# The first attention begins with five of eight projection chunks, and the other three are projected inside its rounds

## The reference, cut to what matters

```
proj = h @ w_in                                   # h: 256 x 1024
qa, kca, vca, ksa, vsa, kwa, vwa, ga, qb, kb, vb = split(proj)
o_a = nsa_attention(qa, kca, vca, ksa, vsa, kwa, vwa, sigmoid(ga), ...)   # compressed + selected + window
o_b = swa_sink_attention(qb, kb, vb, sinks, tab_b)                       # 8 heads, window, sinks
y   = concat(o_a, o_b) @ w_out
```

## Time and profile before

| | us |
|---|---|
| time, median of 3 runs | 1233.58 (1231.28 to 1238.41) |
| time of the profiled execution | 1230.09 |
| its span, first to last instruction | 1228.2 |
| PE busy | 1144.4 |
| DVE busy | 948.5 |
| ACT busy | 602.0 |
| POOL busy | 77.1 |

### The profile page before, as it was taken

How to read it: one execution, slowest core, us unless ns; L and a number is a source line. 1 busy time by engine, 2 the same in 40 slices (tenths; PEclk the granted TensorE clock), 3 DMA queues, 4 the chain that set the end, 5 groups by cost and what they waited for, 6 DMA issues and landing times.

```text
span 1228.2 us, 19517 instructions
## 1 busy us (share of the span) xinstructions
PE 1144.4 (93%) x8036; PEld 1026.6 (84%) x8036; DVE 948.5 (77%) x1638; ACT 602.0 (49%) x1055; POOL 77.1 (6%) x110
## 2 busy tenths in 40 slices
PE   2697899999999998999999999999999979999996
PEld 1696579899997996898998989999989968888885
DVE  5997758888777965788888678897776868777655
ACT  2435755443456457644444664444453265555553
POOL 1020000000000000285000000000000000000000
PEclk9999899999999999999999999999999999999998
DMA  9994235788982951377899637889723542666731
GB/s 374 364 390 166 94 138 194 303 325 283 336 323 72 409 223 58 118 270 261 319 242 361 224 123 285 312 279 330 299 94 119 108 181 88 225 253 259 182 124 35
DMA packets 41097, 280.74 MB, mean 229 GB/s; under 512 B 4768, under 2 KB 5296, under 8 KB 8240
## 3 DMA queue, kind: packets, MB, share of 16 engines
q1 hardware_dynamic: 37584, 269.27, 60.1%
q0 software_dynamic: 2416, 7.92, 2.0%
q10 hardware_dynamic: 1008, 2.30, 0.5%
HBM read 277.85 MB, written 1.10 MB: 227 GB/s over the span
## 4 chain that ended last, share of the span: by engine, by line
PE 72%; DVE 16%; ACT 6%; DMA 4%; issue 1%; SPq 0%; DVEq 0%; ACTq 0%
PE PS L419 71%; DVE LO L1433 5%; DMA raw<-WS 4%; DVE raw L1423 3%; ACT HI L987 2%; ACT SC L987 1%; DVE TMP L1502 1%; DVE HB L1497 1%; ACT SQ L987 1%; PE PS L642 1%; DVE TMP L1539 1%; ACT HB L987 1%; DVE X L1544 1%; DVE TMP L1774 1%; ACT RS L987 0%
## 5 line engine op out<-in xcount | busy, mean ns | idle before, releaser
L419 PE MATMUL PS<-HB,HI 128*128 128x256 f32 (+1 forms) x3160 | 650.3, 299 | 26.1 <-ACT HB L987 18.4
L419 PEld LDWEIGHTS PS<-HB,HI 128*128 128x128 f32 x3160 | 512.0, 193 | 52.5 <-ACT HB L987 20.9
L419 PE MATMUL PS<-HB,LO 128*128 128x256 f32 x1748 | 495.6, 284 | 0.0
L1433 DVE TENSOR_TENSOR LO<-raw,HI 128x1024 fp32r<-128x1024 f32 x340 | 406.1, 1231 | 93.5 <-ACT HI L987 93.2
L987 ACT ACTIVATE HI<-raw 128x1024 fp32r<-128x1024 f32 x340 | 338.4, 1047 | 92.5 <-PE PS L419 48.4
L419 PEld LDWEIGHTS PS<-HB,LO 128*128 128x128 f32 x1748 | 336.5, 193 | 2.9
L1423 DVE CUSTOM_DVE_ANT_0 raw<-raw,CB,SM 128x1024 f32<-128x1024 f32 x168 | 211.5, 1293 | 15.9 <-DMA raw<-WS 15.9
L987 ACT ACTIVATE HDH<-FB 128x256 fp32r<-128x256 f32 x88 | 36.8, 418 | 233.1 <-DVE FB L1621 209.5
L419 PE MATMUL PS<-HI,HDH 128*128 128x512 f32 x352 | 140.2, 398 | 0.0
L419 PE MATMUL PS<-HI,HDL 128*128 128x512 f32 x352 | 139.4, 396 | 0.0
L419 PE MATMUL PS<-LO,HDH 128*128 128x512 f32 x352 | 139.1, 395 | 0.0
(11 more groups left out here) (234 smaller groups left out, 919.9 us busy)
## 6 DMA issues: line engine op xcount, KB each, us to landing
raw<-WS SPq DMA_DIRECT2D x255, 1024.0 KB, 5.4
SC<-scratch POOLq DMA_DIRECT2D x2, 1024.0 KB, 16.3
FB<-gates_out POOLq DMA_DIRECT2D x3, 512.0 KB, 4.5
SQ<-gates_out POOLq DMA_DIRECT2D x3, 512.0 KB, 9.1
X<-xT ACTq DMA_DIRECT2D x1, 1024.0 KB, 6.7
SC<-ssm POOLq DMA_DIRECT2D x2, 512.0 KB, 3.8
out<-TMP SPq DMA_DIRECT2D x4, 256.0 KB, 2.6
CB<-vecs SPq DMA_DIRECT2D x1, 512.0 KB, 6.4
```

The costliest lines, as they stand in the source:

```text
L419: return e.matmul(o, l, r, start=start, stop=stop, skip_group_check=True)
L1433: e.tensor_tensor(LO[:, s % HL, :], raw_half(j, h), HI[:, s % HL, :].bitcast(fp32), O.subtract).then_inc(*D.up(("lo", s)))
```

## The change

Chunks 4, 5 and 6 leave the row of projections. What is begun with is ab 0, 1, 2, 3 and 7; the scores of rounds 0 to 5 need no more. The three others are projected in six halves, `third_set(p)`, in rounds 0 to 5, on PE behind the transposes of that round, into the PSUM banks 2 and 3, which no other step uses at that time. Each of the three engines calls `use(..., 2)` for that half in the round, DVE ahead of `spare` and of its `compressed` functions. The scores of round 6 wait for the new event `third`. The value columns of chunks 6 and 7 change places. In the plan `cmp` moves to place 19, behind ab 7; ab 4, mod 14, ab 5, mod 15, ab 6, mod 16 to 19 and `abo` follow it.

```
-    plan += weave(ws("ab", 8), am[:7], 0) + [("raw", ("cmp", 0))] + am[7:] + ws("abo", 4)
+    plan += weave([("w", ("ab", i)) for i in (0, 1, 2, 3, 7)], am[:6], 0) + [("raw", ("cmp", 0))]
+    for i in (4, 5, 6):
+        plan += [("w", ("ab", i)), am[i + 2]]
+    plan += am[9:] + ws("abo", 4)
...
-                w.wait_ge(*A.at(("fm", tag)))
+                w.wait_ge(*A.at(("fm", tag) if tag == "cd" or p < 6 else "third"))
...
-            for n in range(6):
+            for n in range(4):
                 linear_fm(("ab", n), H2, "ab", 8, 2)
-            keys_values(("ab", 6))
             values_only(("ab", 7))
+
+            def third_set(p):
+
+                key, h = ("ab", 4 + p // 2), p % 2
+                ps = PS[:, 2 + p // 2 % 2, :]
+                wt = [x.rearrange("p (k n) -> p k n", k=8) for x in weight(key, h)]
+                if p == 4:
+                    w.wait_ge(*A.at(("proj", "ab", 4)))
+                if p == 5:
+                    linear_tm(lambda qt: ps[:, 256 + qt * 128:384 + qt * 128], key, 1, range(8), wt, False, True)
+                else:
+                    for k in range(8):
+                        i = mm3(ps[:, h * 256:(h + 1) * 256], [x[:, k, :] for x in wt], H2[k], k, h == 0 and k == 0,
+                                k == 7, "ab")
+                    i.then_inc(*P.up(used(key, h), *([("lin", key, 0)] if h else [])))
...
                 if p > 1:
                     transposes("ab", p - 2)
+                if p < 6:
+                    third_set(p)
                 walk.spare(2)
                 for f in compressed.get(p, ()):
                     f()
... ACT
+            use(("ab", 7), 0, 2)
+            use(("ab", 7), 1, 2)
+            values(("ab", 7), 0, ("fm", "ab"))
+
+            def third_set(p):
+
+                use(("ab", 4 + p // 2), p % 2, 2)
+                ps = PS[:, 2 + p // 2 % 2, :]
+                if p in (1, 3):
+                    w.wait_ge(*P.at(("lin", ("ab", 4 + p // 2), 0)))
+                    fn(flat(FMT[:, p + 3:p + 5, :]), ps, F.Copy, scale=0.125).then_inc(*A.up(("proj", "ab", 4 + p // 2)))
+                if p == 5:
+                    w.wait_ge(*P.at(("lin", ("ab", 6), 1)))
+                    fn(FMT[:, 12, :], ps[:, 0:256], F.Copy).then_inc(*A.up())
+                    fn(VT[:, :, 256:384], ps[:, 256:512].rearrange("p (q n) -> p q n", q=2), F.Copy) \
+                        .then_inc(*A.up("third"))
...
                 for i in (2 * p, 2 * p + 1):
                     exps("ab", i, *AB[i])
+                if p < 6:
+                    third_set(p)
                 high(walk.spare(2))
... DVE
                 if p > 0:
                     scaled("ab", AB, p - 1)
+                if p < 6:
+                    use(("ab", 4 + p // 2), p % 2, 2)
                 low(walk.spare(2))
                 for f in compressed.get(p, ()):
                     f()
```

More of the change, by code:

```diff
@@ L1178, in act @@
             fn(HDH[:, 0, 0:192], S("gate"), F.Copy).then_inc(*A.up("gatew"))
-            for n, i in enumerate((4, 5, 0, 1, 2, 3)):
+            for n, i in enumerate((4, 5, 0, 1)):
                 use(("ab", n), 0)
@@ L1688, in dve @@
                 .then_inc(*D.up("gatew"))
-            for n in range(6):
+            for n in range(4):
                 use(("ab", n), 0)
                 use(("ab", n), 1)
-            for n in (6, 7):
-                use(("ab", n), 0)
-                use(("ab", n), 1)
+            use(("ab", 7), 0, 2)
+            use(("ab", 7), 1, 2)
             w.wait_ge(*P.at("gates2"))
@@ L2277 @@
     r = np.r_
-    abc = [r[512:640, 640:768, 768:896, 1024:1152], pairs, 1304 + pairs, r[1816:1944, 896:1024, 1152:1280, 1944:2072]]
+    abc = [r[512:640, 640:768, 768:896, 1024:1152], pairs, 1304 + pairs, r[1816:1944, 1944:2072, 896:1024, 1152:1280]]
     cdc = [pairs, r[768:1280], r[1280:1792], r[1792:2304], r[512:640, 640:768]]
```

## The result

The changed kernel takes 1243.07 us, median of 6 runs (1241.9 to 1245.58), beside 1234.05 us (1231.28 to 1238.41, 6 runs) for the kernel before. The ratio is 1.007 with an interval of [1.005, 1.0089]: about 9 us slower. The profiled execution took 1245.58 us with a span of 1243.8. An event of one execution also carries scatter: in six kernels that have the same instructions up to `cmp_used` (the changed one, bias_first, filled_wait, spread_mods, spread_and_bias_first and abo_half_moved) the first score begins between 78.7 and 80.9 us and `cmp_used` falls between 98.8 and 101.8.

What follows compares the result with a forecast made beforehand. PE and DVE were taken as full ahead of the attention, a chain of latencies as bounding the rounds. −18.4 + 7.1 + 3.9 + 8.4 + 3.0 = +4.0 us gave 1234.1 profiled, 1237.6 median; range 1228 to 1244.

Steps and rivals of the forecast that it cites:

- the sign of the sum: The five steps up to the end of round 6's scores add to +4.0 us, so slower.
- the likeliest case: Whole kernel follows the five-step schedule: 1237.6 us, own range 1233.5 to 1241.5; chance 0.50.
- Low clock on top: Rival: PE's waits in rounds 4 and 5 put the last projection half at low clock; 1239.5 to 1243, chance 0.20.
- The 3.5 us that I added: Added to the profiled execution's forecast of 1234.1 us to reach the median of the runs, 1237.6.
- Step 1: Start to first score: first score at 78.7 us, 18.4 us earlier than before.
- Step 2: First score to `cmp_used`: 20.4 us, 7.1 more, with three projection halves of 2.9 us on PE.
- Step 3: `cmp_used` to the end of `cmp_bias(0)`: 13.1 us, 3.9 more, with landing, low parts, mod 16 and bias.
- Step 4: To the end of `cmp_bias(1)`: 8.4 us more, six modulation halves 7.25 and a low part 1.15 on DVE.
- Step 5: `cmp_bias(1)` to the end of round 6's scores: 9.9 us, 3.0 more, including the last projection half at 5.3.
- Mod 19 lands by then: In round 4, five chunks behind `cmp_used` land within 15 us; mod 19 is wanted 21 us behind it.
- Behind the rounds: After round 6's scores: no change counted, with bounds 0 and −2.4 us for less DVE work.
- Faster: Rival: only PE's work counts and gaps in the rounds take it; −5 to −10 us, 1224 to 1229, chance 0.15.

Runs made afterwards that it cites:

- bias_first: Changed kernel with DVE's compressed functions of rounds 3 and later put ahead of `use` and `spare`; 1230.14 us, ratio 0.9988.
- filled_wait: Changed kernel with 20 matmuls of 512 columns, result unread, in PE's wait ahead of round 5's transposes; 1235.43 us, ratio 1.0023.
- spread_mods: Changed kernel with two modulation halves ahead of round 4's bias instead of six, four in round 5, no `abo` half in either; 1229.38 us, ratio 0.9981.
- spread_and_bias_first: Changed kernel with the edits of spread_mods and bias_first together; 1228.08 us, ratio 0.996.
- abo_half_moved: Changed kernel with the first `abo` 0 half moved from round 4 to round 5, the six modulation halves staying; 1245.66 us, ratio 1.0062.
- projection_left_out: Changed kernel with the projections of rounds 0 to 5 doing only the first of eight blocks of the feature sum; 1234.54 us, ratio 1.0023.
- modulation_cut_short: Changed kernel with DVE's modulation of mod 14 to 19 reading 16 of 1024 columns; 1242.77 us, ratio 1.0049.
- mods_later_still: spread_and_bias_first with all modulation streamed behind ab 6, and mod 17 to 19 behind `abo` 2; 1228.95 us, ratio 0.9933.

## Why the prediction was right, and where it was off

The time of 1243.07 lies inside the range of 1228 to 1244, at its upper edge, and the sign of the sum was right. But the likeliest case, no difference that can be told, did not come. What came is the likeliest case's schedule with the rival "Low clock on top", to which I gave 0.20 and 1239.5 to 1243. That the time lies inside the range is in part luck. The trace has the output projection 11.9 us later where the sum had 4.0, and 1234.05 + 11.9 would be 1246; the medians differ by less. The 3.5 us that I added for the distance from a profiled execution to the median had no ground in the kernel either: the changed kernel's profiled execution lies 2.5 us above its median.

| step | predicted length, us | measured | off |
|---|---|---|---|
| 1, start to first score | 78.7 | 79.98 | +1.3 |
| 2, to `cmp_used` | 20.4 | 20.86 | +0.5 |
| 3, to the end of `cmp_bias(0)` | 13.1 | 12.54 | -0.6 |
| 4, to the end of `cmp_bias(1)` | 13.6 | 13.52 | -0.1 |
| 5, to the end of the scores of round 6 | 9.9 | 15.78 | +5.9 |

*Step 1* was off by little: chunk 20 landed at 76.32, not 75.4, and 1.3 us is within the scatter of the first score (78.7 to 80.9). That ACT's two high parts stand ahead of the evacuation was right. The gates' transposes waited 1.91 us for ACT, and the first scores then ran at the low clock (2.08 us for 16, where round 2's took 1.16).

*Step 2* had the right size, but I gave it to one cause where there are two. From the first score to the first of the compressed values it takes 17.1 us in the changed kernel. projection_left_out takes 7.6 us of PE's work away and it is still 16.3, with PE waiting for DVE's list (mod 14, ab 5, mod 15 ahead of the bias of pair 2). modulation_cut_short takes the modulation out of that list, and it is still 16.7 with PE's work unchanged. The six kernels with unchanged work there have 16.2 to 18.0. So PE and DVE are nearly equally long, and neither alone shortens the step. No run takes both away.

*Step 3* went as written: ab 6's two low parts, mod 16 and the bias, ending at 113.38.

*Step 4* had the right size and the wrong claim that this is DVE's work alone. "Mod 19 lands by then" was right; what I didn't ask is when the `abo` half in the same call lands. It costs little as long as the modulation covers it (1.1 us, the low part in abo_half_moved), and when the modulation is gone (modulation_cut_short) the step still takes 12.6 us, 7.4 more than the 5.2 of before. bias_first shows the way past both: the bias ahead of the call.

*Step 5* is the step that failed: "transposes 1.15, the last projection half 5.3, compressed transposes 1.2, values and scores 2.2". The order and the wait were right (6.6 us predicted, 4.79 measured, as a low clock in round 4, from 113.8 to 117.2, had made PE itself later). The term that was mis-sized is the last half, 10.28 us instead of 5.3. That is 5.0 of the 5.9 us. The transposes on both sides of it and the values with the scores took 6.2 (from 126.17 to 127.79 and from 138.07 to 142.68) instead of 4.6, and 0.7 came off, since the first of these began ahead of the end of the bias, as soon as L1739 had read its bank. filled_wait shows that this is the clock: with PE kept busy in the wait the step takes 8.7 us and the half 5.4, close to the 5.3 that I had counted. I had let the low level last 3.4 to 6.4 us, as in the earlier trace rows; it lasted from 124.1 to 141.2. The Trainium skill, "TensorE: Matmul & The Clock Gate", "HAM oscillation — how this bites in real kernels", says that a wait for data between bursts makes the next burst begin slow; this trace agrees, with 4.79 us of waiting and then 48 matmuls at 0.214 us each. By that rule alone the likeliest case should have been the slow one.

*Behind the rounds* I counted nothing. The stretch from the scores of round 6 to the output projection got 1.0 us longer (22.4 to 23.4), while its clock is 0.85 instead of 0.92. The chain from the output projection into the next stage has the same pieces, 12.01 us of PE, the high part, the low part, as before (12.05). DVE sat idle for 8.18 us ahead of that low part, where it was 6.87. So the wait of the earlier trace rows stayed: two halves done in advance brought nothing, as predicted.

The output projection begins 11.9 us later, while the medians differ by 9.0. For the twelve kernels the two go together within 4 us (bias_first -1.1 and -2.6, mods_later_still -6.9 and -7.9, abo_half_moved +7.8 and +8.8), so the rounds set most of the result; what single executions add far behind them was not traced to a cause.

The rival "Faster" needed `cmp_bias(1)` at 119.3. spread_mods has it at 118.9 and bias_first at 117.2, and their medians are 3.3 and 2.6 us below before (the interval of bias_first includes no difference), against the 5 to 10 that I had for that case. The gain was too large; in spread_mods a wait ahead of round 4's transposes (3.73 us) stays, and in bias_first waits of 1.45 and 1.56 us.

## What to carry to other kernels

When matmuls are moved out of a full stretch into the gaps of a chain of latencies, look first at what the move does to the other engines' lists: here the loss came from modulation and weight preparation that now stood ahead of a few small bias instructions which free a bank, and from the low clock behind PE's wait for them. Issue the short work on which another engine waits before the long calls that prepare for later. And count a burst of matmuls right behind a wait of several microseconds at half the clock for its whole length: the last half took 10.3 us instead of 5.4 behind waits of 2.74, 4.79 and 5.38 us.

## What was not expected of the hardware

The granted clock stayed at 0.50 for some 15 us of PE work without a gap (126.2 to about 141.2), most of it matmuls with 128 columns of 0.214 us each. In the kernel before, the low level of the earlier trace rows lasted 6.8 us (121.2 to 128.0). In round 4 of the changed kernel PE waited 3.73 us until 112.83, the level fell only at 113.8, when PE was at work again, and it was back at 117.2, under matmuls with 256 columns. What makes the difference was not measured. A wait of 2.74 us (abo_half_moved) was followed by 13.7 us of low clock (123.8 to 137.4), hardly less than the one of 4.79 us, and the compressed values took 3.75 us after a wait of 0.34 us, 6.52 us after one of 2.86.

A chunk of 1 MB landed 9.4 to 11.7 us after it could go out when others were ahead of it (`abo` 0 in modulation_cut_short and ab 4 in the changed kernel), and 6.06 us in the earlier trace rows.
